# One 31-tap convolution tile moved from TensorE to GpSimd in a two-block network kernel

## The chip, the cores and the metric

The kernel runs on one core of one Trainium2 chip. The metric is the device time of one execution in microseconds (us), lower is better. Everything is 32-bit floating point.

## What is computed

A sequence of 256 positions with 1024 channels goes through two blocks of two layers each. The part that the change touches is the "odd mixer" of the first block's second layer. Cut to what matters, with `u` and `gate` of 768 channels and `q` of 256:

```python
z = y @ w_in                                    # [256, 1792]: u 768, gate 768, q 256
u = u * sigmoid(gate)
u = conv1d(u, conv_w, width=31, per channel) + conv_b   # depthwise, padded by 15 on both sides
u = silu(rmsnorm(u) * cnorm_g)
p = pooled(q) @ pool_w * pool_scale
out = concat(u, p) @ w_out
```

Each channel is convolved along the sequence with its own 31 weights. The 768 channels are six tiles of 128 (tile 0 to tile 5), each a block of 128 partitions by 256 positions. Before the mixer lie a normalisation and a feed-forward layer, behind it the projection `o_out`, another feed-forward layer and the whole second block.

## The kernel before

The kernel is written engine by engine, with semaphores between them. Each engine runs its instructions in the order in which they are written. Weights stream through a ring of four slots of 1 MB (`ring`, one DMA issue of SyncE per slot); a stage is a number of slots. The stages around the change are `o_in` (six slots, one per channel tile, giving `u` in one half of a PSUM bank and `gate` in the other), `o_q` (one slot, giving `q` for the pooling) and `o_out` (four slots). Two PSUM banks take turns, so TensorE can be two slots ahead of the engine that empties them. The semaphore `psum_free` counts emptied slots.

For each slot of `o_in` ScalarE takes the sigmoid of the gate (line 1751) and VectorE multiplies it by `u` out of PSUM into the padded tile `u_pad` (line 2571). `released("o_q")`, on which TensorE waits ahead of its part of the convolution (line 1279), is reached with the multiplication of the sixth slot.

The six tiles are convolved by two engines:

- VectorE does tiles 0 to 3, two tiles at a time and their taps in turn (`taps_of_pairs`, `conv_tap`). The first tap is a multiplication with an addition of the bias (line 2552), each of the other thirty a `scalar_tensor_tensor`, `u_acc = u_pad[shifted] * weight + u_acc` (line 2556). Both tensor inputs lie in SBUF. Each waits for the tap before it of the same tile, which is two instructions back. Behind each of the slots 1 to 4 of `o_in` VectorE does 14 taps; the rest follow behind slot 5.
- TensorE does tiles 4 and 5 (`CONV_PE = 2`): a product with a diagonal matrix per tap, 31 products that sum up in PSUM for each tile (line 1283). GpSimd made the diagonal matrices earlier (line 652), beside the feed-forward layers. A 32-bit product of 256 columns is two matmul instructions in the trace.

Behind the convolution TensorE does `o_q` (line 724), then `cn_sum` (line 733): six products with a matrix of ones that sum the squares of all six tiles over the channels. ScalarE makes the squares (lines 1755 and 1764) in the order of `CONV_ORDER`. Then ScalarE takes the root (line 1768), VectorE the reciprocal (line 2582) and the scaling (line 2587), and ScalarE the silu (line 1773). Meanwhile TensorE does the pooling (lines 1294 and 1300), which reads `q_tok`; VectorE copies `q_tok` out of PSUM (line 2580) behind the last tap. ScalarE copies the pooled sums (line 1770) ahead of the silu. TensorE starts `o_out` (line 712) when silu and pooling are there.

GpSimd does nothing between its DMA of `pool_params` (line 664) and its DMA of `rope` (line 667).

```python
squared(0)
squared(1)
for n in range(CONV_PE):
    ...
squared(2)
squared(3)
```

Of the kernel before, what the change touches and what calls it, by code (L numbers as in the profile page):

```python
# [16 lines left out]
ALU = mybir.AluOpType  # L17
ACT = mybir.ActivationFunctionType
AX_X = mybir.AxisListType.X

P = 128
D = 1024
KD = D // P
SEQ = 256
# [3 lines left out]
KR = RW // P  # L28
# [3 lines left out]
CONVW = 31  # L32
# [91 lines left out]
class Steps:  # L124
# [19 lines left out]
    def past(self, name, i=0):  # L144

        if self.known is None:
            return self.sems[name.split(".")[0]], 1
        at, per = self.known[name]
        return self.sems[name.split(".")[0]], (at + per * i if per else at)
# [32 lines left out]
def program(nc, A, known):  # L182
    S = Steps(known)
    step, past = S.step, S.past
    with ExitStack() as ctx:
# [241 lines left out]
        pool_params = arena[:, pool_at:cursor[0]]  # L427
        CONV_PE = 2
        CONV_DVE = KR - CONV_PE
        cursor[0] = arena_floats - CONV_PE * CONVW * P  # L430
        taps = take(CONV_PE * CONVW, P)

# [116 lines left out]
        CONV_BANKS = (2, 3)  # L549
        CONV_ORDER = (0, 1, 4, 5, 2, 3)  # L550

# [38 lines left out]
        def _(pool):  # L590
# [57 lines left out]
            def two_taps():  # L648
                i = 2 * taps_made[0]
                if i < CONV_PE * CONVW:  # L650
                    at = VEC["conv_w"][0] + CONV_DVE * CONVW + i
                    nc.gpsimd.tensor_tensor(taps[:, i:i + 2], ident[:].unsqueeze(1).to_broadcast([P, 2, P]),
                                            vec[:, at:at + 2].unsqueeze(2).to_broadcast([P, 2, P]), ALU.mult) \
                        .then_inc(*step(f"pool.tap{taps_made[0]}"))
                    taps_made[0] += 1
# [7 lines left out]
            pool.wait_ge(psum_free, released("o_in"))  # L663
            pool.dma_start(pool_params, A["pool_params"]).then_inc(pool_in, 16)

            pool.wait_ge(psum_free, released("f2_1_gu"))
# [19 lines left out]
        def _(pe):  # L686
# [592 lines left out]
            pe.wait_ge(psum_free, released("o_q"))  # L1279
            pe.wait_ge(*past(f"pool.tap{CONV_PE * CONVW // 2 - 1}"))  # L1280
            for n in range(CONV_PE):
                for k in range(CONVW):
                    last = mm(ps[:, CONV_BANKS[n], 0:SEQ], taps[:, n * CONVW + k], u_pad[:, CONV_DVE + n, k:k + SEQ],  # L1283
                              start=(k == 0), stop=(k == CONVW - 1))
                last.then_inc(*step(f"pe.conv{n}"))
            linear_tok("o_q", y1)
# [211 lines left out]
        def _(act):  # L1498
# [254 lines left out]
            def squared(k):  # L1753
                act.wait_ge(*past(f"dve.conv{k}_{CONVW - 1}"))
                f(u_sq[:, k], u_acc[:, k], ACT.Square).then_inc(*step(f"act.cn_sq{k}"))

            squared(0)
            squared(1)
            for n in range(CONV_PE):
                k = CONV_DVE + n  # L1760
                act.wait_ge(*past(f"pe.conv{n}"))
                f(u_acc[:, k], ps[:, CONV_BANKS[n], 0:SEQ], ACT.Identity, bias=V("conv_b", k)) \
                    .then_inc(*step(f"act.conv{k}"))
                f(u_sq[:, k], ps[:, CONV_BANKS[n], 0:SEQ], ACT.Square, bias=V("conv_b", k)).then_inc(*step(f"act.cn_sq{k}"))
            squared(2)
            squared(3)
            act.wait_ge(*past("pe.cn_sum"))
# [127 lines left out]
        def _(v):  # L1895
# [662 lines left out]

            taps_of_pairs = [(k + x, i) for k in (0, 2) for i in range(CONVW) for x in (0, 1)]
            begun = 0  # L2560
# [23 lines left out]
            for k in range(KR):  # L2584
                if k >= CONV_DVE:
                    v.wait_ge(*past(f"act.conv{k}"))
                last = stt(u_acc[:, k], u_acc[:, k], V("cnorm_g", k), rs[:, 0], ALU.mult, ALU.mult)
# [439 lines left out]
```

## Time and profile before

| | us |
|---|---|
| median of 3 runs | 3235.11 (3231.88 to 3236.2) |
| the profiled execution | 3232.99 |
| its span on the core | 3231.2 |
| TensorE matmuls busy | 3141.4 (97% of the span) |
| VectorE busy | 2161.2 (67%) |
| ScalarE busy | 572.0 (18%) |
| GpSimd busy | 194.9 (6%) |
| granted TensorE clock, mean | 0.994 of full speed |

Busy time is the time in which an engine has an instruction of its own under way. The times in the rows further down count from the start of the span. The stage around the convolution lies between 1546 and 1626 us.

### The profile page before, as it was taken

How to read it: one execution, taken by the hardware profiler on the slowest of the kernel's cores; microseconds unless marked ns; L12 is line 12 of the kernel's file. 1: busy time of each engine (PE TensorE's matmuls, PEld its weight loads, DVE VectorE, ACT ScalarE, POOL GpSimd, SP SyncE). 2: the span in 40 equal slices, each digit the busy share in tenths (PEclk: the TensorE clock that was granted, in tenths of full speed). 3: DMA queues.
4: the chain of work that ended last, by engine and by line, in shares of the span. 5: the costliest groups of instructions: out<-in, count | busy, mean ns of one | idle time of the engine just before them, and what ended most of it. 6: DMA issues, size and time to landing. Idle time of an engine off the chain costs nothing.

```text
span 3231.2 us, 64048 instructions
## 1 busy us (share of the span) xinstructions
PE 3141.4 (97%) x27762; PEld 2827.7 (88%) x27762; DVE 2161.2 (67%) x4638; ACT 572.0 (18%) x1157; POOL 194.9 (6%) x216
## 2 busy tenths in 40 slices
PE   7999999899999999999999999999999999999998
PEld 3888446588888899999889999999899999999998
DVE  6887437666766477675757657686676576776774
ACT  2000010233333210110121011131110102230111
POOL 1000000122222010000000000010000000000000
PEclk9999999999999999999999999999999999999999
DMA  7456666100000155445344564344444443345343
GB/s 294 169 217 223 236 220 226 53 7 6 7 6 7 66 170 173 167 170 172 118 169 170 173 210 164 121 140 150 152 169 171 144 157 118 131 138 170 134 169 116
DMA packets 69226, 466.41 MB, mean 144 GB/s; under 512 B 7296, under 2 KB 9984, under 8 KB 16217
## 3 DMA queue, kind: packets, MB, share of 16 engines
q1 hardware_dynamic: 51696, 368.07, 32.7%
q0 software_dynamic: 12192, 87.04, 7.3%
q10 hardware_dynamic: 5065, 7.27, 0.8%
q8 instruction: 219, 3.59, 0.4%
q14 instruction: 54, 0.44, 0.0%
HBM read 456.59 MB, written 5.77 MB: 143 GB/s over the span
## 4 chain that ended last, share of the span: by engine, by line
PE 91%; DVE 6%; ACT 1%; DMA 1%; issue 1%; POOL 0%; ACTq 0%; DVEq 0%; SPq 0%; POOLq 0%
PE ps L847 31%; PE ps L1339 18%; PE ps L902 8%; PE ps L712 7%; PE ps L1484 4%; PE ps L926 4%; PE ps L964 1%; PE ps L977 1%; PE ps L983 1%; PE ps L779 1%; PE ps L1358 1%; PE ps L1414 1%; PE ps L1283 1%; PE ps L1388 1%; DMA arena<-in_ada_t 1%; PE ps L749 1%
## 5 line engine op out<-in xcount | busy, mean ns | idle before, releaser
L847 PE MATMUL ps<-arena 128*128 128x128 f32 x4328 | 510.6, 275 | 0.0
L847 PEld LDWEIGHTS ps<-arena 128*128 128x128 f32 x4328 | 496.7, 192 | 0.0
L847 PE MATMUL ps<-arena,ring 128*128 128x128 f32 x2176 | 271.9, 275 | 0.0
L847 PEld LDWEIGHTS ps<-arena,ring 128*128 128x128 f32 x2176 | 258.0, 192 | 0.5
L1995 DVE TENSOR_TENSOR arena<-arena,ps 128x256 f32<-128x256 f32 x143 | 60.2, 421 | 294.0 <-ACT arena L1552 268.0
L2140 DVE CUSTOM_DVE_ANT_0 arena<-arena,vec 128x1024 f32<-128x1024 f32 x168 | 206.5, 1278 | 1.7 <-DMA arena<-in_ada_t 1.7
L1339 PE MATMUL ps<-y,arena 128*128 128x128 f32 x1560 | 191.7, 278 | 5.0 <-DVE arena L1947 5.0
L1339 PEld LDWEIGHTS ps<-y,arena 128*128 128x128 f32 x1560 | 183.0, 194 | 8.8 <-DVE arena L1947 5.2
L1960 DVE TENSOR_TENSOR arena<-ring 128x512 f32<-128x512 f32 (+1 forms) x167 | 111.8, 669 | 64.0 <-DMA ring<-in_w_f_down 32.0
L712 PE MATMUL ps<-arena,ring 128*128 128x512 f32 x352 | 152.2, 592 | 0.0
L712 PEld LDWEIGHTS ps<-arena,ring 128*128 128x128 f32 x352 | 66.9, 190 | 83.8 <-issue 83.7
L1339 PE MATMUL ps<-h,ring 128*128 128x128 f32 x1040 | 128.4, 276 | 0.8 <-ACT h L1881 0.8
L926 PE MATMUL ps<-y,ring 128*128 128x512 f32 (+1 forms) x352 | 123.5, 514 | 3.6 <-ACT y L1534 3.6
L1339 PEld LDWEIGHTS ps<-h,ring 128*128 128x128 f32 x1040 | 124.0, 192 | 3.2 <-issue 1.0
L847 PE MATMUL ps<-y,ring 128*128 128x128 f32 x1008 | 124.5, 276 | 0.0
L1561 ACT ACTIVATE sg<-arena 128x256 f32<-128x256 f32 x107 | 44.6, 417 | 443.9 <-DVE arena L2004 443.9
L847 PEld LDWEIGHTS ps<-y,ring 128*128 128x128 f32 x1008 | 118.6, 192 | 1.1
L926 PEld LDWEIGHTS ps<-y,ring 128*128 128x128 f32 x352 | 68.6, 195 | 57.7 <-issue 53.0
L619 POOL TENSOR_TENSOR arena<-arena 128x512 f32<-128x512 f32 x72 | 95.6, 1334 | 345.0 <-ACT arena L1662 158.0
L1961 DVE TENSOR_TENSOR arena<-ring 128x512 f32<-128x512 f32 (+1 forms) x167 | 114.5, 686 | 0.0
L1969 DVE TENSOR_TENSOR arena<-ring,arena 128x512 f32<-128x512 f32 (+1 forms) x167 | 111.9, 670 | 2.1
L902 PE MATMUL ps<-arena 128*128 128x256 f32 x504 | 112.2, 379 | 0.0
(415 smaller groups left out, 5877.0 us busy)
## 6 DMA issues: line engine op xcount, KB each, us to landing
ring<-in_w_f_gu SPq DMA_DIRECT2D x88, 1024.0 KB, 4.9
arena<-in_ada_t POOLq DMA_DIRECT2D x72, 1024.0 KB, 5.6
ring<-in_w_fx_gu SPq DMA_DIRECT2D x44, 1024.0 KB, 4.9
ring<-in_w_f_down SPq DMA_DIRECT2D x36, 1024.0 KB, 4.8
ring<-in_w_fx_down SPq DMA_DIRECT2D x24, 1024.0 KB, 4.8
ring<-in_w_qk_a SPq DMA_DIRECT2D x18, 1024.0 KB, 4.9
ring<-in_w_qk_r SPq DMA_DIRECT2D x16, 1024.0 KB, 4.9
ring<-in_w_v_r SPq DMA_DIRECT2D x16, 1024.0 KB, 4.8
```

Of the source, the lines that this page charges most:

```text
L619: nc.gpsimd.tensor_tensor(am[:, lev % 2].rearrange("p h c t -> p (h c) t"), n_own[:, u % 2].rearrange("p h c t -> p (h c) t"), mask, ALU.m ...
L712: last = mm(out, w, rhs_, start=(k == 0 and s.opens), stop=(k == kts - 1 and s.closes))
L847: last = mm(out, weights[number][:, j * P:(j + 1) * P], inputs[number](base + j), start=(s.opens and j == 0 and number in (1, 5)), stop=(s ...
L902: last = mm(wide_bank(s)[:, REGION[number]], weights[number][:, j * P:(j + 1) * P], inputs[number](j), start=(j == 0 and number in (1, 5, ...
L926: last = mm(out, ring[:, s.pos, (k * 2 + m) * P:(k * 2 + m + 1) * P], y2(k) if both else y1(k), start=(k == 0), stop=(k == KD - 1))
L1339: last = mm(quarters_bank(s)[:, REGION[number]], *((x, w) if base in ("v_a", "v_r") else (w, x)), start=(j == 0 and number in (1, 5)), sto ...
L1484: last = mm(quarters_bank(s)[:, REGION[number]], weights[number][:, (j - base) * P:(j - base + 1) * P], inputs[number](j), start=(s.opens ...
L1960: tt(both, quarter(s, 2, n), quarter(s, 3, n), ALU.add).then_inc(*step(f"dve.both_{s.key}"))
L1961: tt(own, quarter(s, 0, n), quarter(s, 2, n), ALU.subtract)
L1969: tt(rest, quarter(s, 1, n), less, ALU.subtract).then_inc(weights_summed, 1)
L1995: tt(quad[:, 2:5:2], quad[:, 7:8].to_broadcast([P, 2, P]), banks[:, 1:3], ALU.add) \
L2140: nc.vector.tensor_tensor_reduce(ada_products[:, m % 2], ada_ring[:, n // 2 % ADA_RING, n % 2], cond[:, sgm], 1.0, V("ada_b", 144 * l + 2 ...
```

## The change

The convolution of tile 4 leaves TensorE. VectorE now does tiles 0, 1, 3 and 4, TensorE tile 5 alone, and GpSimd tile 2. GpSimd's first tap is a `tensor_scalar` with multiplication and addition of the bias; each of the other thirty is a `tensor_scalar` multiplication into one of two halves of a new tile `tap_out` and, behind a wait for it, a `tensor_tensor` addition onto `u_acc`: 61 instructions of 128 x 256. GpSimd starts when VectorE has written `u_pad` of tile 2, behind the third slot of `o_in`. Half of the diagonal matrices go away: 16 instructions at line 652 in place of 31. ScalarE's squares are now taken in the order 5, 0, 1, 2, 3, 4, and so are the products of `cn_sum`.

```diff
-        CONV_PE = 2
-        CONV_DVE = KR - CONV_PE
+        tap_out = take(2, SEQ)
+        CONV_POOL, CONV_PE = 2, KR - 1
...
-        CONV_ORDER = (0, 1, 4, 5, 2, 3)
+        CONV_ORDER = (5, 0, 1, 2, 3, 4)
...
             pool.dma_start(pool_params, A["pool_params"]).then_inc(pool_in, 16)
+            pool.wait_ge(psum_free, ST["o_in"].group + CONV_POOL + 3)
+            nc.gpsimd.tensor_scalar(u_acc[:, CONV_POOL], u_pad[:, CONV_POOL, 0:SEQ], V("conv_w", CONVW * CONV_POOL),
+                                    V("conv_b", CONV_POOL), ALU.mult, ALU.add).then_inc(*step("pool.conv0"))
+            for i in range(1, CONVW):
+                nc.gpsimd.tensor_scalar(tap_out[:, i % 2], u_pad[:, CONV_POOL, i:i + SEQ], V("conv_w", CONVW * CONV_POOL + i),
+                                        None, ALU.mult).then_inc(*step(f"pool.times{i}"))
+                pool.wait_ge(*past(f"pool.times{i}"))
+                pool.wait_ge(*past(f"pool.conv{i - 1}"))
+                nc.gpsimd.tensor_tensor(u_acc[:, CONV_POOL], u_acc[:, CONV_POOL], tap_out[:, i % 2], ALU.add) \
+                    .then_inc(*step(f"pool.conv{i}"))
...
-            for n in range(CONV_PE):
-                for k in range(CONVW):
-                    last = mm(ps[:, CONV_BANKS[n], 0:SEQ], taps[:, n * CONVW + k], u_pad[:, CONV_DVE + n, k:k + SEQ],
-                              start=(k == 0), stop=(k == CONVW - 1))
-                last.then_inc(*step(f"pe.conv{n}"))
+            for k in range(CONVW):
+                last = mm(ps[:, CONV_BANKS[0], 0:SEQ], taps[:, k], u_pad[:, CONV_PE, k:k + SEQ],
+                          start=(k == 0), stop=(k == CONVW - 1))
+            last.then_inc(*step("pe.conv"))
...
-            taps_of_pairs = [(k + x, i) for k in (0, 2) for i in range(CONVW) for x in (0, 1)]
+            taps_of_pairs = [(k + x, i) for k in (0, 3) for i in range(CONVW) for x in (0, 1)]
```

## Rows read from the trace of the kernel before

**Rows 1.** The page, part 1: busy time of each engine

```profile
PE 3141.4 (97%) x27762; PEld 2827.7 (88%) x27762; DVE 2161.2 (67%) x4638; ACT 572.0 (18%) x1157; POOL 194.9 (6%) x216
```

**Rows 2.** Chain that ended last, 1520 to 1680 us: start, us, what

```profile
1546.08 34.55 PE ps L712 x160
...
1581.54 27.05 PE ps L1283 x124
1608.59 6.91 PE ps L724 x32
1615.49 2.59 PE ps L733 x12
1618.09 3.61 PE ps L1294 x16
...
1625.80 14.05 PE ps L712 x64
```

**Rows 3.** Timeline of VectorE: start, us, what, [idle before <-releaser]

```profile
1560.68 5.62 DVE L2556 SCALAR_TENSOR_TENSOR arena<-arena,vec 128x256 f32<-128x256 f32 x14
1567.25 0.42 DVE L2571 TENSOR_TENSOR arena<-ps,arena 128x256 f32<-128x256 f32 x1 [0.94 <-ACT arena L1751]
...
1584.42 23.84 DVE L2556 SCALAR_TENSOR_TENSOR arena<-arena,vec 128x256 f32<-128x256 f32 x60
```

**Rows 4.** Timeline of ScalarE, 1609 to 1626 us

```profile
1609.35 0.72 ACT L1755 ACTIVATE arena<-arena 128x256 f32<-128x256 f32 x2
...
1621.72 1.02 ACT L1770 ACTIVATE arena<-ps 64x1024 f32<-64x1024 f32 x1 [3.12 <-PE ps L1294]
1622.76 1.28 ACT L1773 ACT_TABLE_LOAD   x1
1624.05 1.48 ACT L1773 ACTIVATE y<-arena 128x1536 f32<-128x1536 f32 x1
```

**Rows 5.** One line's instructions: duration ns min/median/max, first and last start

```profile
L680 POOL TENSOR_TENSOR arena<-arena x8: 724/790/1052, 2124.9 to 2873.4; 128x256 f32<-128x256 f32 x8
L609 POOL MEMSET arena<- x1: 1837/1837/1837, 474.1 to 474.1; 128x2064 f32 x1
L2721 DVE TENSOR_TENSOR arena<-arena x16: 412/418/947, 2095.9 to 2850.8; 128x256 f32<-128x256 f32 x16
```

**Rows 6.** Timeline of GpSimd and VectorE, 2122 to 2126 us

```profile
2122.82 2.04 POOL L677 TENSOR_TENSOR arena<-arena 128x512 f32<-128x512 f32 x1 [446.44 <-ACT arena L1865]
2124.94 0.79 POOL L680 TENSOR_TENSOR arena<-arena 128x256 f32<-128x256 f32 x1
...
2123.05 0.68 DVE L2717 TENSOR_TENSOR arena<-arena,h 128x512 f32<-128x512 f32 x1
2123.76 1.38 DVE L2720 TENSOR_TENSOR arena<-arena 128x256 f32<-128x256 f32 x1
2125.07 0.94 DVE L2721 TENSOR_TENSOR arena<-arena 128x256 f32<-128x256 f32 x1
```

**Rows 7.** Timeline of both, 1267 to 1269 us

```profile
1267.41 1.12 POOL L652 TENSOR_TENSOR arena<-ident,vec 128x256 f32<-128x256 f32 x1 [31.06 <-DMA ring<-in_w_f_down]
1267.97 1.10 DVE L1961 TENSOR_TENSOR arena<-ring 128x512 f32<-128x512 f32 x1
```

**Rows 8.** Timeline of both, 2147 to 2150 us

```profile
2147.18 2.93 POOL L677 TENSOR_TENSOR arena<-arena 128x512 f32<-128x512 f32 x1 [21.45 <-ACT arena L1865]
...
2147.69 0.68 DVE L2716 TENSOR_TENSOR arena<-arena,h 128x512 f32<-128x512 f32 x1
2148.29 0.68 DVE L2717 TENSOR_TENSOR arena<-arena,h 128x512 f32<-128x512 f32 x1
```

**Rows 9.** Timeline of both, 621 to 624 us

```profile
621.18 2.50 POOL L619 TENSOR_TENSOR arena<-arena 128x512 f32<-128x512 f32 x2 [9.51 <-ACT arena L1662]
...
622.89 1.29 DVE L2424 TENSOR_TENSOR arena<-ps,arena 128x512 f32<-128x512 f32 x2 [3.51 <-PE ps L1135]
```

**Rows 10.** Timeline of TensorE, and one stretch by engine with its granted clock

```profile
1883.50 5.49 PE L1339 MATMUL ps<-y,arena 128*128 128x128 f32 x24 [4.97 <-DVE arena L1947]
...
1882.60:1889.40 6.80, 5.90 (x28) 5.90 (x28) 4.53 (x9) 0.00 (x0) 0.00 (x0) 0.50 0.53 124
```

More of the change, by code:

```diff
@@ L427, in program @@
         pool_params = arena[:, pool_at:cursor[0]]
-        CONV_PE = 2
-        CONV_DVE = KR - CONV_PE
-        cursor[0] = arena_floats - CONV_PE * CONVW * P
-        taps = take(CONV_PE * CONVW, P)
+        tap_out = take(2, SEQ)
+        CONV_POOL, CONV_PE = 2, KR - 1
+        cursor[0] = arena_floats - (CONVW + 1) * P
+        taps = take(CONVW + 1, P)
         hid = arena[:, 0:KF * 512].rearrange("p (k s t) -> p k s t", k=KF, s=2)
@@ L649, in two_taps @@
                 i = 2 * taps_made[0]
-                if i < CONV_PE * CONVW:
-                    at = VEC["conv_w"][0] + CONV_DVE * CONVW + i
+                if i < CONVW:
+                    at = VEC["conv_w"][0] + CONV_PE * CONVW + i
                     nc.gpsimd.tensor_tensor(taps[:, i:i + 2], ident[:].unsqueeze(1).to_broadcast([P, 2, P]),
@@ L1279, in _ @@
             pe.wait_ge(psum_free, released("o_q"))
-            pe.wait_ge(*past(f"pool.tap{CONV_PE * CONVW // 2 - 1}"))
-            for n in range(CONV_PE):
-                for k in range(CONVW):
-                    last = mm(ps[:, CONV_BANKS[n], 0:SEQ], taps[:, n * CONVW + k], u_pad[:, CONV_DVE + n, k:k + SEQ],
-                              start=(k == 0), stop=(k == CONVW - 1))
-                last.then_inc(*step(f"pe.conv{n}"))
+            pe.wait_ge(*past(f"pool.tap{CONVW // 2}"))
+            for k in range(CONVW):
+                last = mm(ps[:, CONV_BANKS[0], 0:SEQ], taps[:, k], u_pad[:, CONV_PE, k:k + SEQ],
+                          start=(k == 0), stop=(k == CONVW - 1))
+            last.then_inc(*step("pe.conv"))
             linear_tok("o_q", y1)
@@ L1753, in squared @@
             def squared(k):
-                act.wait_ge(*past(f"dve.conv{k}_{CONVW - 1}"))
+                act.wait_ge(*past(f"pool.conv{CONVW - 1}" if k == CONV_POOL else f"dve.conv{k}_{CONVW - 1}"))
                 f(u_sq[:, k], u_acc[:, k], ACT.Square).then_inc(*step(f"act.cn_sq{k}"))
[L1757 to L1766, printed above, removed]
+            act.wait_ge(*past("pe.conv"))
+            f(u_acc[:, CONV_PE], ps[:, CONV_BANKS[0], 0:SEQ], ACT.Identity, bias=V("conv_b", CONV_PE)) \
+                .then_inc(*step(f"act.conv{CONV_PE}"))
+            f(u_sq[:, CONV_PE], ps[:, CONV_BANKS[0], 0:SEQ], ACT.Square, bias=V("conv_b", CONV_PE)) \
+                .then_inc(*step(f"act.cn_sq{CONV_PE}"))
+            for k in CONV_ORDER[1:]:
+                squared(k)
             act.wait_ge(*past("pe.cn_sum"))
@@ L2584, in _ @@
             for k in range(KR):
-                if k >= CONV_DVE:
+                if k == CONV_PE:
                     v.wait_ge(*past(f"act.conv{k}"))
```

## The prediction

> **What bounds the kernel now.** I read the busy times first, then the chain of waits around the convolution, then the timeline of each engine there, and last, elsewhere in the trace, what GpSimd and VectorE do to each other. TensorE is busy 97% of the span [rows 1], and in this stage the chain runs through it without a break: 27.05 us of convolution, 6.91 of `o_q`, 2.59 of `cn_sum`, 3.61 of pooling, and then by way of ScalarE to `o_out` at 1625.80 [rows 2]. VectorE is not far behind: its last tap ends at 1584.42 + 23.84 = 1608.26 [rows 3], and `cn_sum` needs its squares. `cn_sum` begins at 1615.49, so VectorE has 7 us to spare, and no more.
>
> **What the change takes from TensorE.** Half of the 27.05 us, 13.5 us. It can't all be kept. With tile 5 alone `o_q` would end near 1602, but the sum needs the squares of tiles 3 and 4, whose last taps VectorE ends at 1608.26 even if nothing disturbs it. So the next thing to be late is VectorE, and how late is the question.
>
> **The tail behind VectorE.** Let T be the end of the last tap. ScalarE's square and the last product of `cn_sum` take some 0.9 us (two squares took 0.72 [rows 4], the twelve instructions of the sum 2.59 [rows 2]). From the first pooling product to `o_out` it was 1625.80 - 1618.09 = 7.7 us, through 3.61 of products, a copy of 1.02, a table load of 1.28 and the silu of 1.48 [rows 2, 4]; VectorE's copy of `q_tok` fits beside the sum. So `o_out` starts at T + 8.7. The kernel before stands at 1625.80, so T = 1617.1 is break-even while TensorE's clock is full. An undisturbed VectorE (T = 1608.3) would give a gain of 8.8 us; that is the most there is.
>
> **GpSimd's own pace.** It starts behind the third slot, when VectorE has written `u_pad` at about 1560.7 [rows 3], and has 61 instructions. An addition of two tiles of this size takes 0.724 us when nothing is beside it, and the wait for its own result before it adds 0.08 (2122.82 + 2.04 = 2124.86, next start 2124.94) [rows 5, 6]. A `tensor_scalar` on GpSimd is nowhere in the trace. It should not cost more than the addition, since it reads one tensor and not two, which makes 0.72 the upper bound; the lower is a fill, which reads none: 1837 ns for 2064 elements is 0.89 ns each, 0.23 us for 256 [rows 5], and I put 0.1 on it as a guess for starting up: 0.33. I take the middle, 0.53. Undisturbed, GpSimd would need 30 x 0.80 + 31 x 0.53 = 40.4 us and end at 1601, ahead of VectorE. The Trainium skill (GPSIMD Engine Reference, Engine selection) calls one-input work on GpSimd roughly line-rate; 256 elements at its 1.2 GHz are 0.21 us, and an estimate from that and 0.1 us of start would put the price at the lower bound, and the sum below about 6 us lower. No row here shows it.
>
> **What they do to each other.** This decides. At 2124.94 GpSimd starts an addition of 256 columns; VectorE's next instruction, also 256 columns and both inputs in SBUF, takes 0.94 us where 0.41 is its normal time [rows 5, 6]. The one before it took 1.38 behind the larger addition [rows 6]. Likewise at 1267.41: GpSimd's instruction takes 1.12 and VectorE's next 1.10, where 0.68 is usual for 512 columns [rows 7, 8]. But where one of VectorE's inputs is in PSUM nothing happens: two such instructions take 1.29 together beside GpSimd's [rows 9]. So two SBUF inputs on VectorE and a reading GpSimd exclude each other, instruction by instruction. The Trainium skill (SBUF — State Buffer, Who interferes with whom) has the same rule, a shared read interface held for the whole instruction; the trace agrees with 0.94 against 0.41. The taps at line 2556 are of this kind: both inputs are in the arena. The work handed to GpSimd therefore isn't beside VectorE's work but between it.
>
> Price: an addition of 0.72 cost VectorE 0.94 - 0.41 = 0.53, its own time less 0.19. I take the same 0.19 off the `tensor_scalar`: 0.34 (0.14 at the lower bound, 0.53 at the upper). Sum: 30 x 0.53 + 31 x 0.34 = 15.9 + 10.5 = 26.4 us (20.2 to 32.3). Against it stand VectorE's idle times of 0.94 before the multiplication of each of the last three slots, of which one stands in [rows 3], 2.8 us, which vanish because VectorE is no longer waiting. T = 1608.3 + 26.4 - 2.8 = 1631.9, and `o_out` at 1640.6: 14.8 us later than before.
>
> **What else moves.** VectorE's multiplications for slots 3, 4 and 5 lie behind 14 taps each, which with GpSimd between them take 14 x (0.40 + 0.43) = 11.7 us in place of 5.62 [rows 3]. The sixth multiplication comes at about 1597 in place of 1581, and TensorE waits for it; convolution and `o_q` then end by 1620, ahead of T. So this wait is hidden behind VectorE, but it and the wait from 1620 to 1632 leave TensorE idle twice for over 10 us. After 4.97 us of idleness its granted clock was 0.50 for 6.80 us, 5.9 of them busy [rows 10], which is 1.2 of 2.4 GHz. Here that would fall on the last product of the sum and the pooling, 3.61 us that become 7.2; ScalarE's copy waits for them. I add 4 us (bounds 0, if the clock holds, and 6, if it also falls in `o_out`). `o_out`: 1644.6, so +18.8.
>
> The diagonal matrices that GpSimd no longer makes lie beside the feed-forward layers, where TensorE runs through; I count them as nothing, and they can take back at most 15 x 0.4 us of VectorE's blocked time that TensorE's products cover. The order of squares costs nothing while ScalarE waits for VectorE anyway. GpSimd's next DMAs wait for a slot of the next feed-forward layer, behind `o_out`, as before. Everything behind `o_out` is moved as a whole.
>
> Sum: the profiled execution took 3232.99; with 18.8 it is 3251.8. The median of the runs is 2.1 us above that execution, so I forecast 3254.
>
> **The rivals.**
>
> *VectorE keeps the port (chance 0.14).* At 2147.18 GpSimd waited through three of VectorE's instructions and got in only when VectorE paused: 2.93 us in place of 1.28; it happened four times, and at 2122.82 it lost one turn, to the instruction at 2123.05 [rows 6, 8]. VectorE's taps run without a pause. Against it: of the nearest shape, 256 columns, GpSimd got its turn each time [rows 6], and so it did at line 652 [rows 7]. If it holds, VectorE ends near 1609, GpSimd does some 5 instructions in the gaps and the rest alone: 1609 + 37 = 1646, then three squares in place of one (0.7 more), and 9.4 + 4 to `o_out` at 1659.4: +33.6, a time of 3269.
>
> *No exclusion for this form (0.09); the faster side.* `scalar_tensor_tensor` with both inputs in SBUF beside GpSimd isn't in the trace, so it may be free of the blocking. Then GpSimd ends at 1601, T stays 1608.3, and the gain is 8.8 us, or 4.8 if TensorE's idle time from 1603 on halves its clock: 3226 to 3230, I say 3228. It decides as soon as each GpSimd instruction costs VectorE less than (1617.1 - 1605.5) / 61 = 0.19 us, or 0.12 with the clock low.
>
> *GpSimd's `tensor_scalar` is dearer than its addition (0.07).* Nothing in the rows excludes that a scalar read from memory slows it. At 1.1 us each, 31 x 0.57 = 18 more than forecast: 3272.
>
> *The bounds within the forecast's case:* with 0.33 us a `tensor_scalar` and a full clock T is 1625.7 and `o_out` starts at 1634.4, +8.6, a time of 3244. With both upper bounds T is 1637.8 and `o_out` starts at 1652.5, +26.7, a time of 3262.
>
> **How the numbers follow.** The forecast's case, alternation with VectorE's tail, has 0.70; its own range is 3244 to 3262. VectorE keeping the port 0.14, the dear multiplication 0.07, no exclusion 0.09. The range goes to 3243 below and to 3270 above: it leaves out the case of no exclusion and most of the dear one. About 0.2%, 6.5 us, is what a measurement of this kernel can tell from no change. The forecast's case, the port kept and the dear one are all slower by more than that: 0.90 with what of the last case is left over. No exclusion splits in two: 0.05 faster, 0.04 between; of the forecast's case 0.01 might end as no change. So faster 0.05, same 0.05, slower 0.90.
>
> **What would show it.** Right: in the trace of the changed kernel line 2556 has two groups of durations, 0.48 us and some 0.9 us, the first lying behind GpSimd's last addition; GpSimd ends before VectorE, near 1612; the sixth multiplication at line 2571 near 1597; VectorE's last tap at 1632; TensorE's granted clock at 0.50 about the pooling. GpSimd's `tensor_scalar` shows its price by its starts. Wrong: taps of 0.48 us throughout, with GpSimd at its own pace (no exclusion), or with GpSimd ending last (port kept). The forecast fails most easily by the price of the `tensor_scalar`, 31 times over, and by who gets the next turn.

## The result, and the profile after

The changed kernel takes 3247.11 us (median of 7 runs; six of them lie between 3242.8 and 3248.32) beside 3234.53 for the kernel before on the same chip: a ratio of 1.0044 [1.0033, 1.0054], slower. The medians are 12.6 us apart, where 18.8 was forecast; the point was 3254 and the range 3243 to 3270. One of its runs, one of the experiment with the sums in PSUM and one of the kernel before in the last session were disturbed (5365, 6229 and 6500 us) and take no part in the ratios. The profiled execution took 3243.97, which is 10.98 more than that of before.

The page, first line and part 1, where TensorE and VectorE answer to [rows 1]:

```profile
span 3242.2 us, 64006 instructions
...
PE 3134.1 (97%) x27700; PEld 2818.8 (87%) x27700; DVE 2179.2 (67%) x4638; ACT 573.1 (18%) x1156; POOL 237.7 (7%) x262
```

TensorE has 7 us less of busy time; VectorE has 18 us more, with the same number of instructions (4638). The chain that ended last, around the convolution, stands against [rows 2]. Columns: start, us, what.

```profile
1561.75 8.00 DVE arena L2562 x14
...
1593.54 32.85 DVE arena L2562 x59
...
1626.41 0.43 ACT arena L1764
...
1626.88 2.08 PE ps L743 x4
1628.95 4.68 PE ps L1303 x16
...
1637.74 15.74 PE ps L722 x64
```

In [rows 2] this stretch ran through TensorE. Now it runs through VectorE's taps (line 2562) for 65 us, from the third slot of `o_in` to the last square, and reaches TensorE only with the last two products of `cn_sum` (line 743). On this trace the whole stage lies 0.98 us later than on that of before, read at the third slot's multiplication (1561.32 against 1560.34), so I take 0.98 off a time before I compare it. VectorE's timeline, against [rows 3]:

```profile
1579.02 9.14 DVE L2562 SCALAR_TENSOR_TENSOR arena<-arena,vec 128x256 f32<-128x256 f32 x14
1588.08 0.41 DVE L2577 TENSOR_TENSOR arena<-ps,arena 128x256 f32<-128x256 f32 x1
...
1593.46 33.31 DVE L2562 SCALAR_TENSOR_TENSOR arena<-arena,vec 128x256 f32<-128x256 f32 x60
```

Fourteen taps take 9.14 us where they took 5.62, the last sixty 33.31 where they took 23.84. The idle time ahead of the last three multiplications is gone, as forecast. The last tap ends at T = 1593.46 + 33.31 = 1626.77, or 1625.8 on the axis of before, where it was 1608.3. GpSimd's timeline in the same stretch:

```profile
1564.67 1.09 POOL L669 TENSOR_SCALAR arena<-arena,vec 128x256 f32<-128x256 f32 x1
1565.84 0.73 POOL L673 TENSOR_TENSOR arena<-arena 128x256 f32<-128x256 f32 x1
1566.55 1.09 POOL L669 TENSOR_SCALAR arena<-arena,vec 128x256 f32<-128x256 f32 x1
...
1618.64 0.72 POOL L673 TENSOR_TENSOR arena<-arena 128x256 f32<-128x256 f32 x1
```

A tap of GpSimd's is two instructions and comes every 1566.55 - 1564.67 = 1.88 us. One line's instructions over the stage (duration min/median/max in ns):

```profile
L2562 DVE SCALAR_TENSOR_TENSOR arena<-arena,vec x120: 470/484/1008, 1555.4 to 1626.3; 128x256 f32<-128x256 f32 x120
...
L669 POOL TENSOR_SCALAR arena<-arena,vec x30: 959/1094/1098, 1562.8 to 1617.5; 128x256 f32<-128x256 f32 x30
...
L673 POOL TENSOR_TENSOR arena<-arena x30: 723/726/987, 1564.0 to 1618.6; 128x256 f32<-128x256 f32 x30
```

The same view of VectorE's taps, cut to one tap of GpSimd's (its multiplication at 1602.41 and its addition at 1603.58 us), holds three:

```profile
L2562 DVE SCALAR_TENSOR_TENSOR arena<-arena,vec x3: 475/693/946, 1601.8 to 1603.2; 128x256 f32<-128x256 f32 x3
```

This pattern repeats. A tap of VectorE's that meets GpSimd's multiplication takes 0.69 us, one that meets the addition 0.95, and the third 0.48, which is the median of the kernel before (478 ns). The starts of undisturbed taps lie 23.84 / 60 = 0.40 us apart [rows 3], since one begins before the last has ended. So a multiplication costs VectorE 0.69 - 0.48 = 0.21 to 0.22 us, and an addition 0.95 - 0.48 = 0.47.

Two windows of VectorE's taps alone, one beside GpSimd and one behind its end (columns: us, busy with count, granted clock, DMA share, GB/s):

```profile
1561.66:1618.63 56.97, 55.06 (x89) 0.93 0.27 93
1618.63:1626.77 8.14, 8.14 (x20) 0.50 0.00 0
```

Beside GpSimd a tap takes 55.06 / 89 = 0.62 us on average, behind it 8.14 / 20 = 0.41. That is the exclusion, and it ends where GpSimd ends. Last, TensorE's timeline, against [rows 2], and its clock in one window (columns: us, then TensorE, weight loads, VectorE, ScalarE, GpSimd busy with counts, granted clock, DMA share, GB/s):

```profile
1588.55 16.10 PE L1292 MATMUL ps<-arena 128*128 128x256 f32 x62 [6.96 <-DVE arena L2577]
...
1619.86 1.22 PE L743 MATMUL ps<-arena,ones 128*128 128x256 f32 x2 [7.01 <-ACT arena L1764]
1626.88 2.08 PE L743 MATMUL ps<-arena,ones 128*128 128x256 f32 x4 [5.80 <-ACT arena L1764]
1628.88 4.74 PE L1303 MATMUL ps<-arena 128*64 128x256 f32 x16
```

```profile
1617.00:1631.00 14.00, 5.34 (x11) 2.89 (x12) 11.87 (x24) 2.99 (x5) 2.28 (x3) 0.52 0.00 0
```

TensorE waits three times, 6.96, 7.01 and 5.80 us. Behind the first wait the 62 instructions of the convolution take 16.10 us, where half of the 27.05 for 124 would be 13.5; behind the third the pooling takes 4.68 (in the chain above) where it took 3.61, and the first slots of `o_out` 15.74 where they took 14.05. The window, around the last two waits, has a granted clock of 0.52, near the 0.50 that is 1.2 of 2.4 GHz.

### The profile page after: what moved, and what is told of

Same layout as the page of the kernel before. It is cut to its first block, busy times and chain, and to the rows that moved or that the text cites. A ratio compares the mean times of both kernels' runs of the same rounds, so it can differ in the third digit from the quotient of the medians.

```text
span 3242.2 us, 64006 instructions
## 1 busy us (share of the span) xinstructions
PE 3134.1 (97%) x27700; PEld 2818.8 (87%) x27700; DVE 2179.2 (67%) x4638; ACT 573.1 (18%) x1156; POOL 237.7 (7%) x262
## 4 chain that ended last, share of the span: by engine, by line
PE 90%; DVE 8%; ACT 1%; issue 1%; DMA 1%; POOL 0%; ACTq 0%; DVEq 0%; SPq 0%; POOLq 0%
PE ps L857 31%; PE ps L1348 18%; PE ps L912 8%; PE ps L722 6%; PE ps L1493 4%; PE ps L936 4%; DVE arena L2562 2%; PE ps L974 1%; PE ps L987 1%; PE ps L993 1%; PE ps L789 1%; PE ps L1367 1%; PE ps L1423 1%; PE ps L1397 1%; PE ps L759 1%; PE ps L1087 1%
```

## The experiments

Each ratio is to the kernel before on the same chip in the same session.

**GpSimd's taps taken out.** GpSimd does only its first tap. This leaves out thirty of the 31 taps of tile 2.

```diff
-            for i in range(1, CONVW):
-                nc.gpsimd.tensor_scalar(tap_out[:, i % 2], ...
-                nc.gpsimd.tensor_tensor(u_acc[:, CONV_POOL], ...
...
-                act.wait_ge(*past(f"pool.conv{CONVW - 1}" if k == CONV_POOL else ...
+                act.wait_ge(*past(f"pool.conv0" if k == CONV_POOL else ...
```

> The changed kernel without GpSimd's sixty instructions of taps 1 to 30; tile 2 gets its first tap only, so thirty taps of it are left out. Theory (GpSimd and VectorE exclude each other while both read SBUF): VectorE's taps are 0.47 us throughout, its last tap ends 17 to 18 us earlier than in the changed kernel (near 1609 in place of 1626.8), and the time falls from 3247 by about 17 us to some 3230, 4 below the kernel before. It also shows what the move off TensorE would be worth if GpSimd's work were free: 8.8 us at most, less what TensorE's clock takes. Rival (VectorE is late because the slots and the pairs of tiles are ordered otherwise, or because TensorE is late): the last tap stays well above 1609 and the time above 3240.

3229.49 us, 0.9994 [0.9984, 1.0003]. VectorE's and TensorE's timelines:

```profile
1584.41 23.84 DVE L2555 SCALAR_TENSOR_TENSOR arena<-arena,vec 128x256 f32<-128x256 f32 x60
...
1608.35 2.08 PE L736 MATMUL ps<-arena,ones 128*128 128x256 f32 x4 [4.53 <-ACT arena L1757]
...
1619.43 15.74 PE L715 MATMUL ps<-y,ring 128*128 128x256 f32 x64 [1.01 <-ACT arena L1520]
```

The taps are back at 23.84 and T at 1608.25, to 0.01 us that of [rows 3]. So VectorE's delay comes from GpSimd's sixty instructions, and not from the new order of tiles. But with half of the convolution gone from TensorE and nothing put in its place, the kernel is not measurably faster. `o_out` starts 6.4 us sooner, of the 8.8 that the forecast gave as the most, since the sum and the pooling behind the wait of 4.53 run at the low clock, and then takes 1.7 longer. What is left by the trace, 4.7 us, is at the edge of the interval.

**Multiplications alone.** This leaves out GpSimd's thirty additions.

```diff
                 pool.wait_ge(*past(f"pool.times{i}"))
-                pool.wait_ge(*past(f"pool.conv{i - 1}"))
-                nc.gpsimd.tensor_tensor(u_acc[:, CONV_POOL], u_acc[:, CONV_POOL], tap_out[:, i % 2], ALU.add) \
-                    .then_inc(*step(f"pool.conv{i}"))
```

> The changed kernel with GpSimd's thirty multiplications but without its thirty additions, which are left out. Theory (only the reading phase excludes VectorE; in the changed kernel's trace a multiplication takes 1.09 us but delays VectorE by only 0.22): last tap at 1606.4 + 30 x 0.22 = 1613, time 3247 - 14 = 3233. Rival (GpSimd's whole busy time excludes VectorE, or the multiplication is the dear part as its duration says): thirty times 0.9, last tap at 1633, time at or above the changed kernel's 3247.

3232.86 us, 0.9998 [0.9988, 1.0008]. GpSimd's and VectorE's lines:

```profile
L669 POOL TENSOR_SCALAR arena<-arena,vec x30: 922/923/1338, 1562.9 to 1593.9; 128x256 f32<-128x256 f32 x30
...
1586.95 25.55 DVE L2559 SCALAR_TENSOR_TENSOR arena<-arena,vec 128x256 f32<-128x256 f32 x60
```

**Additions alone.** This leaves out the multiplications, and adds `u_pad` as it is.

```diff
-                nc.gpsimd.tensor_scalar(tap_out[:, i % 2], u_pad[:, CONV_POOL, i:i + SEQ], ...
-                pool.wait_ge(*past(f"pool.times{i}"))
                 pool.wait_ge(*past(f"pool.conv{i - 1}"))
-                nc.gpsimd.tensor_tensor(u_acc[:, CONV_POOL], u_acc[:, CONV_POOL], tap_out[:, i % 2], ALU.add) \
+                nc.gpsimd.tensor_tensor(u_acc[:, CONV_POOL], u_acc[:, CONV_POOL], u_pad[:, CONV_POOL, i:i + SEQ], ALU.add) \
```

> The changed kernel with GpSimd's thirty additions, which read the padded tile itself, but without its multiplications, which are left out. Theory: an addition reads two tensors and delays VectorE by 0.48, twice what a multiplication does although it is shorter (0.72 us against 1.09): last tap at 1606.4 + 30 x 0.48 = 1620.8, time 3247 - 6 = 3241, dearer than the multiplications alone by some 8 us. Rival (durations decide): cheaper than the multiplications alone.

3235.48 us, 1.0008 [0.9999, 1.0017]: dearer than the multiplications alone by 2.6 us, where some 8 were expected.

```profile
L670 POOL TENSOR_TENSOR arena<-arena x30: 682/704/796, 1563.7 to 1587.5; 128x256 f32<-128x256 f32 x30
...
1595.36 23.83 DVE L2559 SCALAR_TENSOR_TENSOR arena<-arena,vec 128x256 f32<-128x256 f32 x60
```

The two runs price the parts. The base is the T that a VectorE without its three idle times would have, 1608.3 - 2.8 = 1605.5. With multiplications alone T is 1612.50, less the 1.12 by which this trace lies later, 1611.4: 5.9 us for some thirty, 0.20 each. With additions alone it is 1619.19 - 1.79 = 1617.4: 11.9 us, 0.40 each. Together they cost 1625.8 - 1605.5 = 20.3 us, 0.68 per tap of GpSimd's, which is the 0.22 + 0.47 read off the single taps above. The parts add up to 17.8; the other 2.5 lies with the additions. With additions alone the taps of VectorE that meet one have durations of 0.86 and 0.95 us (486/856/953 ns for the 32 taps between 1563 and 1588 us), so an addition costs them 0.38 or 0.47, where in the changed kernel it costs 0.47 throughout. So a multiplication keeps GpSimd busy for 0.92 us, longer than an addition, and yet costs VectorE half as much. The time that GpSimd holds VectorE up is not its duration less a constant. A multiplication reads one tensor and an addition two, and the costs fit that; with two forms measured it is not shown.

The times of the two runs lie less far apart than their T. With additions alone TensorE's last wait is only 1.71 us, and from T to `o_out` it is 1628.14 - 1619.19 = 8.95; with multiplications alone the wait is 6.84 and the stretch 11.62.

The Trainium skill (GPSIMD Engine Reference, Engine selection) calls one-input work on GpSimd roughly line-rate. By the duration, 0.92 us for 256 elements, the runs disagree; the 0.20 to 0.22 us for which VectorE stood is near the 0.21 that an estimate from the page's 1.2 GHz gives.

**VectorE's sums in PSUM.** The running sums of VectorE's four tiles move to two PSUM banks, so that one input of each tap is in PSUM. The rest is as in the changed kernel, apart from the pooling's bank (2 in place of 7) and the squares, which wait for the last tap of their pair.

```diff
+        ACC = {0: ps[:, 3, 0:SEQ], 1: ps[:, 3, SEQ:2 * SEQ], 3: ps[:, 7, 0:SEQ], 4: ps[:, 7, SEQ:2 * SEQ]}
...
-                    stt(u_acc[:, k], u_pad[:, k, i:i + SEQ], V("conv_w", CONVW * k + i), u_acc[:, k], ALU.mult, ALU.add) \
+                    stt(acc_of(k), u_pad[:, k, i:i + SEQ], V("conv_w", CONVW * k + i), acc_of(k), ALU.mult, ALU.add) \
```

> The changed kernel with VectorE's four running sums (tiles 0, 1, 3, 4) in two free PSUM banks in place of SBUF; every VectorE tap then has one input in SBUF and one in PSUM, and nothing is left out. Theory (exclusion only where both of VectorE's tensor inputs are in SBUF): taps of 0.47 us beside GpSimd, last tap near 1609.5; GpSimd unblocked takes 0.93 + 0.08 + 0.72 a tap and ends near 1614, now the last; time 3247 - 12 = 3235, as the kernel before, give or take 3. Rival A (any access of GpSimd to SBUF slows VectorE): last tap stays at 1620 or later, time 3243 or more. Rival B (taps in PSUM are slower in themselves, which eats the gain): taps above 0.5 us even behind GpSimd's last addition.

3230.88 us, 0.9997 [0.9988, 1.0006], against 1.0044 for the changed kernel. The taps and GpSimd's two lines:

```profile
L2566 DVE SCALAR_TENSOR_TENSOR ps<-arena,vec,ps x120: 478/481/484, 1554.5 to 1607.5; 128x256 f32<-128x256 f32 x120
...
L673 POOL TENSOR_SCALAR arena<-arena,vec x30: 917/922/926, 1561.2 to 1610.8; 128x256 f32<-128x256 f32 x30
...
L677 POOL TENSOR_TENSOR arena<-arena x30: 721/725/731, 1562.2 to 1611.8; 128x256 f32<-128x256 f32 x30
```

With the same work on every engine, no tap takes more than 0.484 us, and GpSimd's durations have no spread either. This is the plainest evidence for the exclusion, and for [rows 9], which had it from two instructions. The Trainium skill (SBUF — State Buffer, Who interferes with whom) has the same rule, that a VectorE instruction with two SBUF inputs contends with a GpSimd instruction that reads SBUF; a greatest value of 484 ns here against 1008 in the changed kernel agrees. That the interface is held for the whole instruction, as the prediction takes it from there, these runs don't bear out: VectorE loses 0.22 us to a multiplication that keeps GpSimd busy for 0.92. Now GpSimd is last, at 1612.5, by its own pace, and TensorE waits 9.82 us for it. The first slots of `o_out` take 17.04, and no gain is measured.

**The kernel before with GpSimd's work added.** TensorE convolves tiles 4 and 5 and VectorE tiles 0 to 3, as before; GpSimd convolves tile 2 as well, into a tile that nothing reads. Nothing is left out.

```diff
+        tap_out = take(2, SEQ)
+        u_spare = take(SEQ)
...
+            for i in range(1, CONVW):
+                nc.gpsimd.tensor_scalar(tap_out[:, i % 2], u_pad[:, 2, i:i + SEQ], ...
...
+                nc.gpsimd.tensor_tensor(u_spare, u_spare, tap_out[:, i % 2], ALU.add) \
```

> The kernel before, with TensorE still convolving tiles 4 and 5, and GpSimd doing the changed kernel's 61 instructions of tile 2 beside it into a tile that nobody reads. Nothing is left out. Theory: VectorE's last tap goes from 1608.3 to about 1626 as in the changed kernel, and since the sum waits for it, the time is the changed kernel's within 3 us, 3244 to 3250: taking half of the convolution off TensorE is worth nothing once VectorE is blocked. Rival (part of the loss is hidden behind TensorE's longer convolution, or TensorE's idle time and low clock are a large part of it): 3241 or less. TensorE is idle less here, so the clock's part of the loss is smaller by some 2 to 4 us.

3241.01 us, 1.003 [1.002, 1.0041]. VectorE's and TensorE's timelines:

```profile
1594.48 33.33 DVE L2568 SCALAR_TENSOR_TENSOR arena<-arena,vec 128x256 f32<-128x256 f32 x60
...
1589.56 28.86 PE L1295 MATMUL ps<-arena 128*128 128x256 f32 x124 [6.96 <-DVE arena L2583]
...
1627.92 1.13 PE L745 MATMUL ps<-arena,ones 128*128 128x256 f32 x4 [0.87 <-ACT arena L1767]
1628.98 3.67 PE L1306 MATMUL ps<-arena 128*64 128x256 f32 x16
...
1636.76 8.44 PE L724 MATMUL ps<-y,ring 128*128 128x256 f32 x38 [1.01 <-ACT arena L1530]
```

T is 1627.81 - 2.00 = 1625.8, that of the changed kernel, though TensorE does both tiles. TensorE's whole convolution fits in front of VectorE's end, so relieving it is worth nothing. With it TensorE works almost up to the last two products (its wait is 0.87 us), the pooling takes 3.67, and from T to `o_out` it is 8.95 us where the changed kernel needs 10.97. The time is below the 3244 to 3250 that was expected, but the kernel before, measured beside it, is faster too, 3231.17; 9.8 us above that is the lower end of what was expected. The trace lacks the part of the changed kernel's loss that comes from TensorE's idle time. By the times alone that isn't shown, since the intervals of the two ratios overlap.

**TensorE kept busy, with the sums in PSUM.** Unread 128-column products are put in ahead of the wait for GpSimd's square.

```diff
+                if i == 3:
+                    for _ in range(40):
+                        mm(ps[:, 5, 0:P], ones[:], blk[:], start=True, stop=True)
```

> The variant with VectorE's running sums in PSUM, and in addition forty products that nobody reads, put into TensorE's wait between the third and the fourth product of the sum, to keep its clock. Theory: in that variant the first o_out slots took 17.0 us in place of 14.05 because the granted clock was low; with the clock kept they take 14.05, and the time falls by 3 to 4 us, from 3231 to about 3228. Rival (the clock costs nothing that counts, or the added products delay the sum): the same or more.

3229.62 us, 0.9995 [0.9985, 1.0004]. TensorE's timeline, and its clock in `o_out`:

```profile
1606.65 9.09 PE L1303 MATMUL ps<-blk,ones 128*128 128x128 f32 x80
...
1618.24 3.67 PE L1312 MATMUL ps<-arena 128*64 128x256 f32 x16
...
1626.02 17.08 PE L726 MATMUL ps<-y,ring 128*128 128x256 f32 x64 [1.02 <-ACT arena L1536]
...
1625.00:1632.00 7.00, 5.98 (x15) 4.85 (x15) 0.88 (x2) 0.86 (x2) 0.00 (x0) 0.52 0.00 0
```

The pooling is at full speed, but the low clock has not gone; it came later, behind the pauses of 1.11 and 1.02 us, and fell on `o_out`. No gain beyond the noise, where 3 to 4 us were expected. The same two pauses stand in the kernel before, and there `o_out` took 14.05 [rows 2], so they alone don't bring the low clock.

**Multiplications on ScalarE.** As before this one, but ScalarE makes the first tap and the products, into eight tiles, and GpSimd only adds; the squares are taken in the order 5, 2, 0, 1, 3, 4, with 22 unread products in place of 40.

```diff
-                nc.gpsimd.tensor_scalar(tap_out[:, i % 2], u_pad[:, CONV_POOL, i:i + SEQ], ...
+                pool.wait_ge(*past(f"act.times{i}"))
...
+                        f(tap_out[:, i % 8], u_pad[:, CONV_POOL, i:i + SEQ], ACT.Copy,
+                          scale=V("conv_w", CONVW * CONV_POOL + i)).then_inc(*step(f"act.times{i}"))
```

> VectorE's running sums in PSUM, the multiplications of tile 2 made by ScalarE (eight tap buffers), only the thirty additions by GpSimd, the square of tile 2 taken early, and 22 unread products in TensorE's wait for the last squares. Nothing is left out. Theory: GpSimd does an addition every 0.80 us and ends near 1587, blocks nobody, VectorE's last tap at 1608 is what comes last, o_out starts at 1617 in place of 1625.8, and the time is 8 to 9 us below the kernel before: about 3224. Rival (ScalarE's taps delay the sigmoids of the next slots and with them VectorE, or GpSimd waits for ScalarE): o_in's slots later by a microsecond or more each, and a time at the kernel before's 3232 or above.

3223.28 us, 0.9979 [0.997, 0.9988], faster than the kernel before.

```profile
1563.14 26.01 POOL L673 TENSOR_TENSOR arena<-arena 128x256 f32<-128x256 f32 x30 [21.44 <-ACT arena L1774]
...
1618.80 17.04 PE L722 MATMUL ps<-y,ring 128*128 128x256 f32 x64 [1.02 <-ACT arena L1532]
```

GpSimd is done at 1589.15, and VectorE, undisturbed, is last. `o_out` still starts into the low clock.

**The changed kernel again**, to have it beside the next two.

> The changed kernel once more, unchanged, beside the variants of this call, so that differences of a few microseconds can be read within one session. Theory and rivals alike: a ratio to the kernel before of 1.0033 to 1.0054, as first measured. Against the kernel before with GpSimd's unread work (ratio 1.0030): if TensorE's low clock is part of the loss, it is 3 to 4 us above that one.

3247.45 us, 1.0048 [1.0035, 1.0062]: the same time. But the low clock lies elsewhere in this trace, which at the stage is 1564.06 - 1560.34 = 3.72 us later than that of before:

```profile
1631.57 5.17 PE L1304 MATMUL ps<-arena 128*64 128x256 f32 x16
...
1640.85 14.05 PE L723 MATMUL ps<-y,ring 128*128 128x256 f32 x64 [1.02 <-ACT arena L1528]
```

T is 1629.46 (the last sixty taps start at 1596.18 and take 33.28) less 3.72, 1625.7, as in the first trace. From T to `o_out` it is 11.39 us, and `o_out` takes its full-speed 14.05. So one and the same kernel loses 1.7 us in `o_out` in one execution and nothing in another, and a reading of the clock from a single trace holds for that execution alone.

**The changed kernel with TensorE kept busy** in all three waits. The kernel is otherwise the changed one.

```diff
+            for _ in range(28):
+                mm(ps[:, 7, 0:P], ones[:], blk[:], start=True, stop=True)
             pe.wait_ge(psum_free, released("o_q"))
...
+                for _ in range({3: 30, 4: 25}.get(i, 0)):
+                    mm(ps[:, 7, 0:P], ones[:], blk[:], start=True, stop=True)
```

> The changed kernel with products that nobody reads in TensorE's three waits (28 before the convolution, 30 and 25 between the products of the sum); nothing is left out. Theory: the granted clock stays full over the pooling and o_out, the pooling takes 3.67 us in place of 4.74, the two last products of the sum 1.1 in place of 2.1, o_out's first slots 14.05 in place of 15.74, together 3 to 4 us: a time 3 to 4 us below the changed kernel's, still some 10 above the kernel before. Rival (the clock falls a little later, as it did in the variant with forty products): 1 to 2 us. VectorE's last tap must stay where it is in both.

3242.43 us, 1.0029 [1.0019, 1.004]: 5.0 us less by the medians. The two intervals overlap, but every execution (3236.7 to 3243.7) is below every one of the changed kernel's in the same session (3246.0 to 3248.4). VectorE's and TensorE's timelines:

```profile
1594.54 33.31 DVE L2568 SCALAR_TENSOR_TENSOR arena<-arena,vec 128x256 f32<-128x256 f32 x60
...
1629.52 3.67 PE L1309 MATMUL ps<-arena 128*64 128x256 f32 x16
```

VectorE's taps are the same 33.31. The pooling is back at full speed, and T to `o_out` is 1637.30 - 1627.85 = 9.45 us in place of 10.97; the 0.5 above 8.95 is about the time by which the added products overrun T. `o_out` takes 15.74 here. Against the first trace of the changed kernel that is 1.5 us less up to the end of `o_out`'s first slots, against the second, which has 11.39 and 14.05, only 0.2. So the 5.0 us are clear of the noise, but the traces don't show them in this stage, and where they come from stays open.

**ScalarE's multiplications, and the last two pauses filled.** The kernel with the multiplications on ScalarE, and five unread products behind each half of the pooling.

```diff
             last.then_inc(*step("pe.pool"))
+            for _ in range(5):
+                mm(ps[:, 0, 0:P], ones[:], blk[:], start=True, stop=True)
...
             last.then_inc(*step("pe.pool_w"))
+            for _ in range(5):
+                mm(ps[:, 0, 0:P], ones[:], blk[:], start=True, stop=True)
```

> The fastest variant so far (ScalarE's multiplications, running sums in PSUM, 22 unread products) with five more unread products before each of the two waits behind the pooling. Nothing is left out. Theory: the low clock that made o_out's first slots 17.04 us in place of 14.05 came from the pauses behind the pooling; with them filled it is gone, and the time is 3 us lower, 3220. Rival (it depends on something else than these pauses): the same time as that variant, 3223.

3222.3 us, 0.9972 [0.9961, 0.9982], the fastest kernel of all, and nothing is left out in it.

```profile
1619.35 13.98 PE L722 MATMUL ps<-y,ring 128*128 128x256 f32 x64
```

`o_out` takes 13.98 in place of 17.04, 3.06 us less. The median is only 1.0 us below that of the kernel without the ten products, which was measured in another session, and the two intervals overlap, so that gain isn't shown by the times. Nor does one trace of each show that the filled pauses did it, since the changed kernel had 15.74 and 14.05 in two executions with the same pauses.

**The multiplication with a second operation.** The changed kernel; GpSimd's `tensor_scalar` adds 0.0.

```diff
-                                        None, ALU.mult).then_inc(*step(f"pool.times{i}"))
+                                        0.0, ALU.mult, ALU.add).then_inc(*step(f"pool.times{i}"))
```

> The changed kernel with GpSimd's thirty multiplications written as multiplication and addition of zero, like its first tap; the result is the same and nothing is left out. In the variant with sums in PSUM the first tap, which multiplies and adds, took 0.54 us and the thirty that only multiply 0.92 each. If the form decides, each now takes 0.54 unblocked. Theory (what GpSimd reads blocks VectorE, not how long it is busy): GpSimd ends some 10 us sooner, VectorE's last tap stays where it is within 2 us, time 3247 within 2. Rival (busy time blocks): last tap 30 x 0.38 = 11 us sooner, time near 3236. Third possibility: the first tap was short only because it came first; then nothing changes.

3243.34 us, 1.0039 [1.0024, 1.0054], which can't be told from the changed kernel.

```profile
L669 POOL TENSOR_SCALAR arena<-arena,vec x30: 517/648/652, 1563.2 to 1606.0; 128x256 f32<-128x256 f32 x30
...
1597.88 28.55 DVE L2562 SCALAR_TENSOR_TENSOR arena<-arena,vec 128x256 f32<-128x256 f32 x60
```

The multiplication takes 0.65 us in place of 1.09, and GpSimd ends at 1606.2 in place of 1618.4, both on the axis of before (this trace lies 1.37 us later). T is 1626.43 - 1.37 = 1625.1, against 1625.8. GpSimd's own pace hardly matters to VectorE: the taps that meet a multiplication and an addition still take 0.69 and 0.94 us, but there are two of VectorE's to each of GpSimd's in place of three. What each instruction takes away stays the same, and only comes in a shorter stretch.

**The same form with the sums in PSUM.**

```diff
-                                        None, ALU.mult).then_inc(*step(f"pool.times{i}"))
+                                        0.0, ALU.mult, ALU.add).then_inc(*step(f"pool.times{i}"))
```

> The same form in the variant with VectorE's sums in PSUM; nothing is left out. If the form decides: GpSimd's pace per tap 1.33 us in place of 1.71, its end 11 us sooner, near 1601, VectorE's last tap at 1608 last; o_out some 4 us sooner and the time 3227 in place of 3231. If not: 3231.

3224.86 us, 0.998 [0.997, 0.999], faster than the kernel before.

```profile
L673 POOL TENSOR_SCALAR arena<-arena,vec x30: 469/478/485, 1563.6 to 1600.3; 128x256 f32<-128x256 f32 x30
...
1622.15 15.74 PE L726 MATMUL ps<-y,ring 128*128 128x256 f32 x64 [1.01 <-ACT arena L1531]
```

GpSimd ends at 1601.6 us and VectorE at 1610.5. VectorE is last again and undisturbed, which is what the change needed from the start.

## Why the prediction was right, and where its sizes were off

**The exclusion, in turns.** Right. VectorE's taps have three kinds of duration, 0.48, 0.69 and 0.95 us, where the forecast named two, and the long ones end with GpSimd's last addition. VectorE keeping the port would have shown GpSimd last and T near 1609; no exclusion would have shown T at 1608.3. The trace has neither, and the taps in PSUM take the cause away and the effect with it.

**The price of it.** The forecast took 0.53 us an addition and 0.34 a multiplication, 26.4 in all, and T = 1631.9. Measured are 0.47 and 0.22 on the single taps of the changed kernel (0.40 and 0.20 when each kind stands alone), 20.3 us in all, and T = 1625.8. The step that was mis-sized is "its own time less 0.19". It came from one pair of instructions [rows 6], and made of GpSimd's duration a measure of what it blocks. For the addition it was near, 0.53 against 0.47. The multiplication refutes it in both directions: 0.92 us long it would have cost 0.73, and it cost 0.22; shortened, it cost no less.

**The duration of the `tensor_scalar`.** Wrong, outside its bounds of 0.33 and 0.72: 0.92 us undisturbed, 1.09 beside VectorE. "It should not cost more than the addition, since it reads one tensor and not two" was an argument without a row, and the rival that had it dear, by that rule, at 3272 had the duration nearly right and the consequence wrong. The two errors offset each other: a longer instruction that blocks less. That was luck. With the right duration the forecast's own rule gives 30 x 0.53 + 31 x 0.73 = 38.5 us in place of 26.4, and a time near 3266, almost 20 us too high. GpSimd's end came at 1618.4 on the axis of before, where 1612 was forecast. The sixth multiplication came at 1587.1 where I had 1597, as the stages of `o_in` hold three groups of 14 taps at 8.1 to 9.1 us each, not 11.7; the wait that it causes was hidden, as forecast.

**TensorE's relief.** Right that it can't be kept, and too mild: it is worth nothing. The kernel before with GpSimd's work added has the same T, at a ratio of 1.0030 [1.002, 1.0041] against 1.0044 and 1.0048 for the changed kernel. To the end of `o_out`'s first slots it needs 23.0 us from T, the changed kernel 26.7 in one trace and 25.4 in the other. So by the traces TensorE's idle time costs 2.4 to 3.7 us, and the convolution that it is spared gives nothing.

**The tail and the clock.** From T to `o_out` I had 8.7 us and 4 for the low clock, 12.7. At full clock it is 8.95. In the changed kernel's first trace it is 10.97, and `o_out` takes 1.7 longer, so the low clock costs 3.7 us, 1.7 of them in `o_out`, which I had only in the bounds. In its second trace it is 11.39 with nothing lost in `o_out`: 2.4 us, all of it where I had put it. The size was right in one execution and too high in the other.

**The sum.** `o_out` starts at 1636.76 on the axis of before, 10.96 later than at 1625.80, and takes 1.7 more: 12.7 us, beside 12.6 between the medians. The forecast had 18.8, and 6.1 of the difference of 6.2 is T. That is the first trace; by the second, `o_out` is 11.3 us later and no longer, so the agreement with the medians to 0.1 us is in part chance. The two profiled executions are 10.98 apart and not 12.7 + 0.98, because the clock fell at other places in one than in the other. Instruction for instruction, VectorE's starts lie 13.6 us later up to 1886 us on the axis of before, 12.6 from 1891, 9.6 from 2327, 7.9 from 2550 and 10.9 from 3000. The step at 2327 is this (the first line is the kernel before, the second the changed one; the columns are those of the window from 1617 to 1631 us):

```profile
2310.00:2340.00 30.00, 26.59 (x174) 23.57 (x174) 18.96 (x36) 9.32 (x17) 0.00 (x0) 0.89 0.21 72
2320.00:2350.00 30.00, 26.58 (x197) 24.33 (x196) 21.14 (x40) 9.34 (x17) 0.00 (x0) 1.00 0.23 76
```

There the kernel before ran at a granted clock of 0.89 and the changed one at 1.00. The second trace of the changed kernel has none of these steps: it lies 15.0 us later from 1712 to the end. So single executions differ by steps of 1 to 3 us in stages that the change doesn't touch, and two profiled executions can't be compared by their ends.

## What to carry to other kernels

Before work goes to GpSimd beside VectorE, look for VectorE instructions with two SBUF inputs in that stretch; if there are any, the work isn't beside but between, and one of the inputs put into PSUM takes the exclusion away at no cost (a tap of 481 ns against 478 undisturbed in SBUF). Before an engine is relieved, ask which engine ends next: here VectorE ended only 7 us before TensorE began the sum, and a relief without any price (the run without GpSimd's taps) gave 2.6 us by the medians, with an interval from 1 us lost to 5 gained. A TensorE that waited for 4.5 us or more ahead of the last products of the sum lost some 2 to 4 us in the clock of what followed, and not always at the same place; with last waits of 0.87 and 1.71 us it lost none.

## What the runs showed of the hardware

- A `tensor_scalar` on GpSimd with one operation and a scalar per partition took 0.92 us for 128 x 256, and with a second operation (`+ 0.0`) 0.48, both undisturbed; the addition of two tensors took 0.72. Why the shorter program is the slower I can't say.
- GpSimd holds VectorE up for a part of its instruction: 0.22 us of a multiplication that takes 0.92 undisturbed, 0.47 of an addition's 0.72. Shortened to 0.48 us by the second operation, the multiplication still costs 0.22.
- `scalar_tensor_tensor` with the running sum in PSUM took 481 ns, in SBUF 478 (median, the kernel before), so the move itself was free.
- Unread products in a wait of TensorE's kept the clock over the pooling (3.67 us), but in the trace taken it then fell in `o_out` (17.08 us); with the pauses of 1.11 and 1.02 us filled too, `o_out` took 13.98. One execution of each was traced, and the changed kernel itself had 15.74 in one and 14.05 in another, so that filling these pauses keeps the clock is not shown.
